# One encoder layer on one core: the last tile of the second norm in halves, and the first up pair's units in row order

## The reference

```python
mix = concatenate([o_att, o_hg]) @ w_out
x = x + g1 * rms_norm(mix, norm_mix_post)

h = rms_norm(x, norm_ffn_pre) * (1.0 + sc2) + sh2
u = h @ w_up                       # 2048 -> 2 * 5632
u = depthwise_conv3(u) + conv_b
a, b = split(u, 2)
y = (gelu(a) * b) @ w_down
x = x + g2 * rms_norm(y, norm_ffn_post)
```

## Time and profile before

| | us |
|---|---|
| median of three runs | 2387.89 |
| lowest, highest run | 2387.69, 2389.78 |
| span of the profiled execution (the profile gives no other time for it) | 2387.6 |
| TensorE busy | 2305.7 (97%) |
| VectorE busy | 1890.5 (79%) |
| ScalarE busy | 1101.9 (46%) |

### The profile page before, as it was taken

One profiled execution on the slowest core, in us unless ns is written; L12 is line 12 of the kernel. 1 busy time (PEld: TensorE's weight loads), 2 busy tenths in 40 slices (PEclk: granted clock), 3 DMA queues, 4 the chain that ended last, 5 costly groups with the idle time before them and its releaser, 6 DMA issues.

```text
span 2387.6 us, 36981 instructions
## 1 busy us (share of the span) xinstructions
PE 2305.7 (97%) x13613; PEld 2029.3 (85%) x13613; DVE 1890.5 (79%) x2417; ACT 1101.9 (46%) x1495; POOL 111.3 (5%) x185
## 2 busy tenths in 40 slices
PE   2899999999999999989999999999999999999997
PEld 2777778888888877878999999999999998888886
DVE  6865767877767873267899999999999998889898
ACT  5366753333333353254444444444444445555554
POOL 1010000000000000000000000000000000000000
PEclk9999999999999999989999999999999999999998
DMA  9952456766666724336555555555555569756574
GB/s 370 324 158 72 147 178 194 230 221 211 209 213 194 232 94 168 98 123 162 142 146 144 141 143 145 145 144 143 143 143 143 142 189 326 246 187 198 187 250 175
DMA packets 371312, 430.91 MB, mean 180 GB/s; under 512 B 14268, under 2 KB 291012, under 8 KB 368928
## 3 DMA queue, kind: packets, MB, share of 16 engines
q1 hardware_dynamic: 354704, 369.74, 49.1%
q0 software_dynamic: 16528, 60.15, 10.3%
HBM read 407.27 MB, written 54.54 MB: 193 GB/s over the span
## 4 chain that ended last, share of the span: by engine, by line
PE 90%; DVE 5%; ACT 2%; DMA 2%; issue 1%; SPq 0%; DVEq 0%; ACTq 0%
PE bank L2014 27%; PE bank L2015 27%; PE bank L2016 27%; PE bank L2171 2%; DMA ADA<-in_w_ada_dram 1%; PE bank L2080 1%; PE bank L2203 1%; DVE ACC L1327 1%; PE bank L2190 1%; PE bank L2071 1%; PE bank L2233 1%; DVE ZZ L1515 0%; DVE W_lo L1281 0%; PE bank L2009 0%; DVE X L1957 0%
## 5 line engine op out<-in xcount | busy, mean ns | idle before, releaser
L2014 PE MATMUL bank<-H_lo,W_hi 128*128 128x256 f32 (+1 forms) x1888 | 659.8, 349 | 3.3 <-DVE H_lo L1342 3.3
L2015 PE MATMUL bank<-H_hi,W_hi 128*128 128x256 f32 (+1 forms) x1888 | 635.0, 336 | 0.0
L2016 PE MATMUL bank<-H_hi,W_lo 128*128 128x256 f32 (+1 forms) x1888 | 635.0, 336 | 0.0
L2014 PEld LDWEIGHTS bank<-H_lo,W_hi 128*128 128x128 f32 x1888 | 359.9, 191 | 42.5 <-issue 7.7
L2015 PEld LDWEIGHTS bank<-H_hi,W_hi 128*128 128x128 f32 x1888 | 360.0, 191 | 39.4 <-issue 7.7
L2016 PEld LDWEIGHTS bank<-H_hi,W_lo 128*128 128x128 f32 x1888 | 359.3, 190 | 37.8
L2014 PE MATMUL bank<-T_lo,W_hi 128*128 128x256 f32 x1280 | 362.2, 283 | 0.0
L2015 PE MATMUL bank<-MGR,W_hi 128*128 128x256 f32 x1280 | 362.2, 283 | 0.0
L2016 PE MATMUL bank<-MGR,W_lo 128*128 128x256 f32 x1280 | 362.2, 283 | 0.0
L1281 DVE TENSOR_TENSOR W_lo<-W_raw,W_hi 128x1024 fp32r<-128x1024 f32 x138 | 168.2, 1220 | 107.0 <-ACT W_hi L727 106.6
L2014 PEld LDWEIGHTS bank<-T_lo,W_hi 128*128 128x128 f32 x1280 | 245.8, 192 | 0.0
(11 more groups left out here) (279 smaller groups left out, 3619.5 us busy)
## 6 DMA issues: line engine op xcount, KB each, us to landing
AB_raw<-in_w_ada_dram SPq DMA_DIRECT2D x128, 512.0 KB, 4.5
UB<-in_w_up_dram SPq DMA_DIRECT2D x100, 512.0 KB, 4.1
W_raw<-in_w_in_dram SPq DMA_DIRECT2D x90, 512.0 KB, 4.6
t_dram<-in_w_down_dram POOLq DMA_DIRECT2D x66, 512.0 KB, 7.7
DRAW<-in_w_down_dram SPq DMA_DIRECT2D x66, 512.0 KB, 4.3
W_raw<-in_w_up_dram SPq DMA_DIRECT2D x56, 512.0 KB, 4.0
W_raw<-in_w_down_dram SPq DMA_DIRECT2D x44, 512.0 KB, 4.6
ADA<-in_w_ada_dram SPq DMA_DIRECT2D x32, 512.0 KB, 5.7
```

Of the source, the lines that this page charges most:

```text
L2014: pe.matmul(acc, st_hi, mv_lo, start=start, stop=False)
L2015: pe.matmul(acc, st_hi, mv_hi, start=False, stop=False)
L2016: return pe.matmul(acc, st_lo, mv_hi, start=False, stop=stop)
```

## The change

Tile 3's residual is computed in two column halves, each counted by `x1_ready`. ScalarE squares the left half when it is there, turns its sum into `sum/D + eps` with an Identity, squares the right half when that is there, and takes the root with the first as its bias. VectorE scales tile 1 ahead of tile 3's sum, where it split UP; the split of UP goes behind all scalings. ScalarE splits UP and UP+1 both ahead of tile 3's square. UP+2 is split by VectorE at row 2 and UP+3 at row 4 (before, behind the scalings and at row 3). The units of the first pair are loaded in another order: UP is a with rows 0 to 7, UP+1 b with rows 0 to 7, UP+2 and UP+3 the same with rows 8 to 15, and `up_row` picks them so; `unit_used` is counted after rows 7 and 15 of each half. The last store waits for both halves, and the first convolution's wait counts one unit more.

```diff
--- before.py
+++ after.py
@@ -273,6 +273,7 @@
     CS, S1, S2, LBV, LBC, EPSC = 0, 16, 32, 48, 64, 80
     SSX, RSX, SSM, RSM, SS2, RS2 = 81, 85, 89, 105, 109, 113
     SSY, RSY, QNS, QNSR, LBT = 117, 133, 137, 138, 144
+    SS2H = 139
     PMX, PSM, PRC = 144, 148, 152
     GC = 192
 
@@ -420,6 +421,7 @@
             return [PB[(0 if jj % 2 else 4) + n] for n in range(4)]
 
         left, right = slice(0, 256), slice(256, 512)
+        left_half, right_half = slice(0, D // 2), slice(D // 2, D)
 
 
 
@@ -542,12 +544,13 @@
                     u = j * 4 + U_UP + k
                     sp.wait_ge(lo_ready, u - RAW + 1)
                     sp.dma_start(W_raw[:, k % 2, :].rearrange("p (t n) -> p t n", n=P),
-                                 half_tile(w_up, j * P + (k // 2) * D_FF, k % 2)).then_inc(raw_landed[k % 2], 16)
+                                 half_tile(w_up, j * P + (k // 2 if j else k % 2) * D_FF, k % 2 if j else k // 2))\
+                        .then_inc(raw_landed[k % 2], 16)
 
             load_up(0)
 
             for tt in range(TT):
-                sp.wait_ge(x1_ready, tt + 1)
+                sp.wait_ge(x1_ready, tt + 1 if tt < TT - 1 else TT + 1)
                 sp.dma_start(x1_dram[tt * P:(tt + 1) * P, :], XR[:, tt, :]).then_inc(x1_stored, 16)
             for j in range(1, PLAIN):
                 load_up(j)
@@ -1058,20 +1061,30 @@
 
             def x1_norm(tt):
                 act.wait_ge(x1_ready, tt + 1)
-                after(act.activation(JO[:, :], XR[:, tt, :], ACT.Square, accum_out=col(SM, SS2 + tt)))
-                act.activation(col(SM, RS2 + tt), col(SM, SS2 + tt), ACT.Sqrt, bias=col(SM, EPSC), scale=1.0 / D)\
+                if tt < TT - 1:
+                    after(act.activation(JO[:, :], XR[:, tt, :], ACT.Square, accum_out=col(SM, SS2 + tt)))
+                    act.activation(col(SM, RS2 + tt), col(SM, SS2 + tt), ACT.Sqrt, bias=col(SM, EPSC), scale=1.0 / D)\
+                        .then_inc(x1_rms, 1)
+                    return
+
+
+                after(act.activation(JO[:, left_half], XR[:, tt, left_half], ACT.Square, accum_out=col(SM, SS2 + tt)))
+                act.activation(col(SM, SS2H), col(SM, SS2 + tt), ACT.Identity, bias=col(SM, EPSC), scale=1.0 / D)
+                act.wait_ge(x1_ready, TT + 1)
+                after(act.activation(JO[:, right_half], XR[:, tt, right_half], ACT.Square, accum_out=col(SM, RS2 + tt)))
+                act.activation(col(SM, RS2 + tt), col(SM, RS2 + tt), ACT.Sqrt, bias=col(SM, SS2H), scale=1.0 / D)\
                     .then_inc(x1_rms, 1)
 
             for tt in range(TT):
                 if tt == TT - 1:
                     split_hi(0, 4, U_UP)
+                    split_hi(0, 4, U_UP + 1)
                 out_squares(3, [tt])
                 act.wait_ge(mix_summed, tt + 1)
                 act.activation(col(SM, RSM + tt), col(SM, RSM + tt), ACT.Sqrt, bias=col(SM, EPSC), scale=1.0 / D)\
                     .then_inc(mix_rms, 1)
                 if tt:
                     x1_norm(tt - 1)
-            split_hi(0, 4, U_UP + 1)
             x1_norm(TT - 1)
             split_hi(0, 4, U_UP + 2)
             for kt in range(KT):
@@ -1094,7 +1107,7 @@
                 jj = j + half * FT
                 if bank is None:
                     bank = PB[2 * e + half]
-                    act.wait_ge(unit_used, n * 2 + (U_UP + 2))
+                    act.wait_ge(unit_used, n * 2 + (U_UP + (2 if n else 3)))
                 else:
                     act.wait_ge(posted, (j - PLAIN) * 7 + (7 if half else 5))
                 if not (isinstance(j, int) and j < 2):
@@ -1648,13 +1661,13 @@
                 dve.wait_ge(x1_rms, tt + 1)
                 after(dve.reciprocal(col(SM, RS2 + tt), col(SM, RS2 + tt)))
 
-                for cols in (slice(0, D),) if tt < TT - 1 else (slice(0, D // 2), slice(D // 2, D)):
+                for cols in (slice(0, D),) if tt < TT - 1 else (left_half, right_half):
                     dve.tensor_scalar(MG[:, tt, cols], XR[:, tt, cols], col(SM, RS2 + tt), None, ALU.mult).then_inc(x1_scaled, 1)
 
             dve.wait_ge(xr_landed, 16 * TT)
             for tt in range(TT):
                 if tt == TT - 1:
-                    split_lo(0, 4, U_UP)
+                    scale_x1(1)
                 dve.wait_ge(mg_squared, 3 * TT + tt + 1)
                 dve.tensor_reduce(col(SM, RSM + tt), SM[:, SSM + 4 * tt:SSM + 4 * tt + 4], AX.X, ALU.add)\
                     .then_inc(mix_summed, 1)
@@ -1664,15 +1677,17 @@
                 dve.wait_ge(mix_rms, tt + 1)
                 after(dve.reciprocal(col(SM, RSM + tt), col(SM, RSM + tt)))
                 dve.wait_ge(mg_ready, 3 * TT + tt + 1)
-                dve.scalar_tensor_tensor(XR[:, tt, :], MG[:, tt, :], col(SM, RSM + tt), XR[:, tt, :], ALU.mult, ALU.add)\
-                    .then_inc(x1_ready, 1)
-            scale_x1(1)
+                for cols in (slice(0, D),) if tt < TT - 1 else (left_half, right_half):
+                    dve.scalar_tensor_tensor(XR[:, tt, cols], MG[:, tt, cols], col(SM, RSM + tt), XR[:, tt, cols],
+                                             ALU.mult, ALU.add).then_inc(x1_ready, 1)
             scale_x1(TT - 2)
             scale_x1(TT - 1)
+            split_lo(0, 4, U_UP)
             split_lo(0, 4, U_UP + 1)
-            split_lo(0, 4, U_UP + 2)
             for kt in range(KT):
-                if kt == 3:
+                if kt == 2:
+                    split_lo(0, 4, U_UP + 2)
+                if kt == 4:
                     split_lo(0, 4, U_UP + 3)
                 dve.wait_ge(h2_ready, kt + 1)
                 if kt % 2:
@@ -2322,18 +2337,15 @@
                 pe.wait_ge(h2_lo, kt + 1)
                 w = slice((kt % 8) * P, (kt % 8 + 1) * P)
                 for half in range(2):
-                    u = U_UP + 2 * half + kt // 8
+                    u = U_UP + half + 2 * (kt // 8)
                     slot = u % SLOTS
                     if kt % 8 == 0:
                         pe.wait_ge(lo_ready, u + 1)
                     pe.matmul(PB[half][:, :], W_hi[:, slot, w], H_lo[:, kt, :], start=(kt == 0), stop=False)
-                    mid = pe.matmul(PB[half][:, :], W_hi[:, slot, w], H_hi[:, kt, :], start=False, stop=False)
+                    pe.matmul(PB[half][:, :], W_hi[:, slot, w], H_hi[:, kt, :], start=False, stop=False)
                     ins = pe.matmul(PB[half][:, :], W_lo[:, slot, w], H_hi[:, kt, :], start=False, stop=(kt == KT - 1))
 
-                    if half == 0 and kt % 8 == 7:
-                        ins.then_inc(unit_used, 1)
-                    if half == 1 and kt == KT - 1:
-                        mid.then_inc(unit_used, 1)
+                    if kt % 8 == 7:
                         ins.then_inc(unit_used, 1)
 
             for kt in range(KT):
```

## The result

| | before | changed |
|---|---|---|
| median, lowest to highest (9 runs each) | 2390.04, 2387.69 to 2392.56 | 2397.29, 2393.26 to 2400.03 |
| ratio of the changed kernel to the one before, 95% interval | | 1.0024 (1.0015 to 1.0033) |
| span of the profiled execution | 2387.6 | 2395.5 |

The change makes the kernel slower, by about 0.24%, which is the ratio that was forecast (the plain ratio of the two medians is 1.0030, within the interval). The time itself, 2397.29, lies 1.9 us above the range. The two medians are 7.25 us apart, where 5.8 was forecast, and the kernel before, measured with it, came out at 2390.04 and not at 2387.89.

What follows compares the result with a forecast made beforehand. TensorE, busy for 97% of the span, was taken to bound the kernel. Span 2387.6 + 5.3 (wait for the late load) + 0.5 (clock) = 2393.4, plus 0.3 from span to median: 2393.7 us, range 2392.1 to 2395.4.

Steps and rivals of the forecast that it cites:

- The mechanism: Before `up_row(0)`: UP+2's load goes out 8.3 us late, ScalarE waits for it, TensorE starts 5.3 us later.
- The chain before it: Tile 3's sum, residual, square and root up to its reciprocal, before the transposes: rebuilding it gains 0.2 us.
- Unit order and halves: First up pair's load order costs nothing; halving tile 3's residual costs VectorE 0.13 us within a 0.2 us gain.
- signs of being wrong: `h2_row(0)` before 1050, TensorE making up time after 1060, or transposes starting over 0.5 us away from 1045.8.
- the base of the sum: Whole kernel: profiled span of 2387.6 us, with the median of the runs taken as 0.3 us above it.
- The stall: TensorE before `up_row(0)`: start at 1054.9 against 1049.58, +5.3 us, taking 4.0 us for UP+2's load.
- The clock's term: TensorE's restart at half clock after the new pause: +0.5 us, bounds -0.25 and +1.3.
- The load was in the way: Rival at ScalarE's split of UP+2 said the opposite: load landed in time, 2387.7, no change; chance 4%.
- the transposes keep the clock's rise: Rival before `up_row(0)`: clock rises near 1053.8 within the pause, saving 2.1 us, 2391.1; chance 4%.
- The second wait, for UP+3: Rival at row 3: UP+3's load, among stores, holds ScalarE up to 3 us, 2394.7; chance 4%.
- an estimate of 3.2 us: UP+2's load of 512 KB: 2.0 us fixed plus bytes at 436 GB/s, making the 5.3 us term 4.5.

Runs made afterwards that it cites:

- the late splits: Changed kernel with UP+2 and UP+3 split at rows 4 and 6 on ScalarE, 5 and 7 on VectorE: 2389.24, ratio 1.0004 to the kernel before.
- filled kernels: Identity transposes added in TensorE's pauses: kernel before 0.9997, changed kernel with both pauses 1.0016, changed kernel with UP+2 and UP+3 split later 1.0004.

## Why the prediction was right and where it failed

**The mechanism** was right. The load of UP+2 went out 9.48 us after the last output matmul (forecast 1047.58 - 1038.16 = 9.42), ScalarE stood 7.26 us before its split (forecast 6.8), TensorE got a second pause, nothing was made up later. Undoing either half of the cause removes the loss: wholly with the load early (ratio 0.9998), but for a wait of 1.74 us with ScalarE's split moved (1.0007). The chain before it was right too: tile 3's reciprocal at 6.70 us, forecast 6.66, before 6.89. Unit order and halves cost nothing, as forecast. One of the prediction's own signs of being wrong did appear: the transposes were to start within 0.5 us of 1045.8 and started at 1047.51, and the load was to go out near 1047.6 and did so at 1049.28. Both are the 1.6 us from ahead of the seam. Counted from the last output matmul the transposes came at 7.71 us, forecast 7.64. In a kernel whose first part moves by more than that from one execution to the next, such signs have to be counted from an event close by.

**The step that failed is the base of the sum.** The prediction said that "the median of the runs is 0.3 above the span", and added 0.3 to a sum made from the span. But each run of the changed kernel is listed with its span, and the time is 1.8 to 2.1 us above it (2397.51 beside 2395.5). In the 79 later runs of the kernel before it is 1.7 to 1.8 us (2389.46 beside 2387.7, 2388.68 beside 2386.9). The profile with 2387.6 therefore belongs to a time near 2389.4, and the median of three, 2387.89, lay near the floor of a kernel that ranges from 2386.8 to 2392.4 over 33 runs in one session. Of the 3.6 us by which 2397.29 misses 2393.7, this base is 2.15 (2390.04 against 2387.89); the other 1.45 are the loss itself, 7.25 against 5.8.

The part of the program ahead of the seam shows why runs spread so: the last output matmul ended anywhere from 1036.3 to 1039.8 us in eleven profiles without filling, though the code ahead of it is the same. Below are the kernel before and then the changed kernel, each with the row of a wait near 175 us and the clock around it.

```profile
176.72 0.47 PE L2014 MATMUL bank<-K_lo,Q_hi 128*128 128x512 f32 x1 [2.04 <-DVE Q_lo L1441]
172.00:178.00 6.00, 3.96 (x18) 1.00 0.15 34
178.00:184.00 6.00, 6.00 (x30) 1.00 0.69 187
```

```profile
176.58 0.47 PE L2029 MATMUL bank<-K_lo,Q_hi 128*128 128x512 f32 x1 [2.04 <-DVE Q_lo L1454]
172.00:178.00 6.00, 3.96 (x16) 0.92 0.16 36
178.00:184.00 6.00, 6.00 (x23) 0.80 0.68 182
```

TensorE waits 2.0 us near 175 in both. In the changed kernel's profile the clock fell over it (0.80 in 178 to 184), in the other it did not. Up to here the two are within 0.14 us of each other, and the last output matmul is 1.6 us later. The second profile of the changed kernel, the earliest of all, had the full clock both here and over 120 to 126 us (1.00, against 0.80 in its first profile). A range that hung on three runs had to be wider on this account alone; 2392.1 to 2395.4 should have been centred about 2 us higher, and would then have taken in 2397.29.

**The size of the loss** was a little short. The stall came to 5.74 and 5.40 us in the two profiles (forecast 5.3), because the transfer took 4.44 and 4.11 us from issue to ScalarE's split, where 4.0 was taken and 4.3 was the upper bound. The clock's term was 0.5 us with bounds -0.25 and +1.3; the profiles give 0.2 against the kernel before itself and 0.9 against all six without the second pause. By them the seam costs 5.7 to 6.5 us, against 5.8 forecast. The medians say 7.25, the ratio on record 5.7, with its interval 3.6 to 7.9 us. Some 0.2 us is that the changed kernel's times stand further above their spans; the rest of the gap is not explained by anything in the traces, and with a spread of 5 us among runs it need not be. That the measured ratio is the forecast 1.0024 to the last digit is luck at this spread.

**The rivals.** The load was in the way. That the transposes keep the clock's rise had been given 4% and did happen in a sense: with ScalarE's split at row 2, with the early and with the late splits the rise fell ahead of row 0. In the changed kernel's first profile it rose in the second pause, and was down again before row 0 at 1056.96, so it gave nothing:

```profile
1048.00:1050.00 2.00, 2.00 (x11) 0.50 0.00 0
1051.00:1053.00 2.00, 0.00 (x0) 1.00 0.90 253
1055.00:1057.00 2.00, 0.04 (x1) 0.50 1.05 430
```

The second wait, for UP+3, did not occur. The Trainium skill's page TensorE: Matmul & The Clock Gate (section Why this matters for your kernels), with its warning against gaps between bursts, agrees with the traces in that the second pause left no free restart in four profiles of four; but four of the seven without that pause had none either, so these traces don't single out the second gap. The Trainium skill's page DMA: Bandwidth & Descriptors (section Anatomy of one DMA — SWDGE (gpsimd) path), whose fit gives an estimate of 3.2 us, was further off than the rows: 3.85 to 4.44 us here.

## What to carry to other kernels

When a step is moved on one engine, look up which loads its counter releases, and then what stands behind the consumer of that load on its own in-order engine: here a 1.1 us split moved 8 us later held up the first rows of the up projection by 5.4 to 5.7 us. If the new order makes an operand needed later, move all its handling with it, and not the consumer's half alone. And before a small absolute difference is forecast, ask how the profiled span stands to that execution's own time and how far runs of the same kernel spread, for three runs say little about either.

## What the hardware showed that I had not expected

Transposes of 128x128 in the pause ran at full clock (64 in 7.15 us), and the clock stayed up while they lasted, yet it still fell for about 3 us behind the short waits that follow them, in all three filled kernels. Filling a pause with them was worth nothing in the kernel before (ratio 0.9997). And at a pause of 2.0 us near 175 us the clock fell in five of the eleven profiles without filling and not in the other six. With the pauses near 60 and 112 us, behind which it also came back sooner in some executions, the seam moves by up to 3.6 us.
